# Fused two-block transformer kernel, fp32, one core: first modulation third in the gate-up chunks, gate's steps sooner, shared rotated key as ninth unit, first input tile in halves

## The reference

```python
# first block, DEPTH = 2 times
z = rms_norm(x, g_mix_pre) @ w_in                # 1024 x 3200: rq rk rv rg aq ak av gu gv
y = concat(silu(rg) * retention(rope(rq), rope(rk), rv),
           dilated_attention(rope(aq), rope(ak), av),
           gelu(gu) * (tril(w_s) @ group_norm(gelu(gv)) + b_s))      # "the gate"
x = x + rms_norm(y @ w_out, g_mix_post)
gate, up = split(rms_norm(x, g_ffn_pre) @ w_gate_up)                 # 2816 + 2816 columns
x = x + rms_norm((silu(gate) * up) @ w_down, g_ffn_post)
# second block, l = 0 (even) and l = 1 (odd); the same for ctx, with c_ctx
sh, sc, g = split(silu(c) @ w_mod[l] + b_mod[l], 3)                  # three thirds of 1024
h = rmsnorm(x, norm_g[l]) * (1 + sc) + sh
y = even_layer(h) if l == 0 else odd_layer(h)
x = x + g * y
```

## Time and profile before

| | |
|---|---|
| timed runs, us | 1135.35, 1136.14, 1138.33 |
| profiled execution, us | 1137.99 |
| its span, us | 1136.2 |
| mean granted TensorE clock | 0.986 |
| TensorE (PE) busy | 1085.5, 96% |
| VectorE (DVE) busy | 688.2, 61% |
| ScalarE (ACT) busy | 551.1, 49% |
| GpSimd (POOL) busy | 77.3, 7% |
| moved by DMA | 170.46 MB, mean 150 GB/s |
| chain that ended last | PE 81%, DVE 10%, ACT 4%, issue 3%, DMA 2% |

### The profile page before, as it was taken

One profiled execution on the slowest core, in us unless ns is written; L12 is line 12 of the kernel. 1 busy time (PEld: TensorE's weight loads), 2 busy tenths in 40 slices (PEclk: granted clock), 3 DMA queues, 4 the chain that ended last, 5 costly groups with the idle time before them and its releaser, 6 DMA issues.

```text
span 1136.2 us, 15595 instructions
## 1 busy us (share of the span) xinstructions
PE 1085.5 (96%) x5974; PEld 890.5 (78%) x5974; DVE 688.2 (61%) x1206; ACT 551.1 (49%) x990; POOL 77.3 (7%) x94
## 2 busy tenths in 40 slices
PE   7789999999999989999999999999998999999997
PEld 5588968888886788967888778889796678789785
DVE  5577576666546487575666547523256753876664
ACT  5435455555435435455555445334235742524772
POOL 1000010000001000020000000001000002022040
PEclk9889999999999999999999999999999999999999
DMA  9654467565665754468755485223221011444000
GB/s 333 229 157 135 130 222 241 176 180 183 186 186 195 283 189 131 138 213 278 230 176 181 149 333 150 77 88 103 74 70 42 1 57 56 130 127 133 1 2 38
DMA packets 109572, 170.46 MB, mean 150 GB/s; under 512 B 7213, under 2 KB 70714, under 8 KB 109242
## 3 DMA queue, kind: packets, MB, share of 16 engines
q1 hardware_dynamic: 107424, 161.92, 44.9%
q0 software_dynamic: 1440, 6.10, 1.5%
q10 hardware_dynamic: 634, 1.44, 0.3%
HBM read 168.39 MB, written 1.05 MB: 149 GB/s over the span
## 4 chain that ended last, share of the span: by engine, by line
PE 81%; DVE 10%; ACT 4%; issue 3%; DMA 2%; SPq 0%; DVEq 0%; POOLq 0%; POOL 0%; ACTq 0%
PE PS L478 15%; PE PS L479 15%; PE PS L480 15%; PE PS L2974 4%; PE PS L2975 4%; PE PS L2976 4%; DVE low L451 2%; PE PS L978 2%; DMA raw<-w_in 1%; PE PS L1811 1%; ACT high L441 1%; PE PS L940 1%; PE PS L941 1%; PE PS L942 1%; PE PS L1918 1%
## 5 line engine op out<-in xcount | busy, mean ns | idle before, releaser
L451 DVE TENSOR_TENSOR low<-raw,high 128x1024 fp32r<-128x1024 f32 (+3 forms) x182 | 202.0, 1116 | 224.1 <-ACT high L441 223.5
L478 PE MATMUL PS<-high,hT_high 128*128 128x512 f32 (+2 forms) x796 | 309.6, 389 | 7.8 <-DVE low L451 5.5
L441 ACT ACTIVATE high<-raw 128x1024 fp32r<-128x1024 f32 (+3 forms) x186 | 180.2, 975 | 271.4 <-PE PS L480 148.7
L479 PE MATMUL PS<-low,hT_high 128*128 128x512 f32 (+2 forms) x796 | 301.5, 379 | 0.0
L480 PE MATMUL PS<-high,hT_low 128*128 128x512 f32 (+2 forms) x796 | 301.3, 378 | 0.0
L478 PEld LDWEIGHTS PS<-high,hT_high 128*128 128x128 f32 x796 | 151.8, 191 | 49.1 <-issue 11.4
L480 PEld LDWEIGHTS PS<-high,hT_low 128*128 128x128 f32 x796 | 151.9, 191 | 24.2
L479 PEld LDWEIGHTS PS<-low,hT_high 128*128 128x128 f32 x796 | 152.1, 191 | 22.1
L454 DVE SCALAR_TENSOR_TENSOR low<-raw,vec_cols,high 128x512 fp32r<-128x512 f32 x176 | 124.2, 747 | 51.7 <-ACT high L444 51.7
L444 ACT ACTIVATE high<-raw,vec_cols 128x512 fp32r<-128x512 f32 x176 | 117.0, 714 | 46.6 <-PE PS L480 44.7
L2974 PE MATMUL PS<-high,fT_high 128*128 128x512 f32 x176 | 70.4, 400 | 0.0
(11 more groups left out here) (378 smaller groups left out, 1613.7 us busy)
## 6 DMA issues: line engine op xcount, KB each, us to landing
raw<-w_gate_up SPq DMA_DIRECT2D x176, 256.0 KB
raw<-w_mod SPq DMA_DIRECT2D x48, 512.0 KB
raw<-w_down SPq DMA_DIRECT2D x44, 512.0 KB
raw<-w_in SPq DMA_DIRECT2D x56, 384.0 KB
raw<-o_w_in SPq DMA_DIRECT2D x20, 512.0 KB
raw<-w_out SPq DMA_DIRECT2D x16, 512.0 KB
raw<-e_w_in SPq DMA_DIRECT2D x12, 512.0 KB
raw<-w_in SPq DMA_DIRECT2D x8, 512.0 KB
```

The lines of the kernel that those rows point to most:

```text
L441: last = e.activation(g.high, g.raw, ACT.Copy)
L451: last = e.tensor_tensor(g.low, g.raw, g.high.bitcast(F32), ALU.subtract)
L478: e.matmul(bank, xh[:, k, tokens], g.high[:, i, :], start=first and i == 0, stop=False)
L479: e.matmul(bank, xh[:, k, tokens], g.low[:, i, :], start=False, stop=False)
```

## The change

- The first third of a layer leaves the mixer. Its eight pieces stand singly in the gate-up chunks, one behind each of the four pieces of chunk 2 (`c` = 0) and of chunk 4 (`c` = 1), ScalarE's copies in chunks 3 and 5, the columns at chunk 6, the bias in chunk 7 (MOD_AT).
- The mixer's steps for the gate move forward on ScalarE and VectorE, and aq's low parts move behind the ropes of ak.
- The shared rotated key is turned as the ninth of 17 units and spread while the rest is copied; the cuts of y's pieces 2 and 3 move from step 1 to step 3.
- Piece 2 of the odd layer's first chunk is cut ahead of the context's last tile.
- At the start x's first tile comes in two loads and is taken by halves, the gains from place 5 on are loaded by SyncE, a small activation on ScalarE stands ahead of its other loads, and the positions are worked out after the first pieces.

```diff
-        MOD_AHEAD = {7: (0, 0), 8: (0, 1), 10: (1, 0), 11: (1, 1)}
+        MOD_AT = {(2, h): (0, h) for h in range(4)} | {(4, h): (1, h) for h in range(4)}
...
-                for rows in PAIRS:
+                for h, rows in enumerate(PAIRS):
+                    if (c, h) in MOD_AT:
+                        of, n = MOD_AT[c, h]
+                        add_mod(layer, 0, (of,), PAIRS[n:n + 1])
                     w_gu[layer].add_split(a["w_gate_up"][layer], rows, c * SEQ, SEQ, pre_gain(V_FFN, layer, rows))
...
@@ def mix_step_pe @@
-            if s in MOD_MIX:
-                if s == 6 and where.layer == 0:
-                    e.wait_ge(dve.sem, dve.value("silu_c"))
-                    e.wait_ge(dve.sem, dve.value("wsT"))
-                c, half = MOD_MIX[s]
-                mod_rows_pe(e, 0, c, slice(2 * half, 2 * half + 2))
-            elif s == 11:
+            if s == 11 and where.layer == 0:
+                e.wait_ge(dve.sem, dve.value("wsT"))
+            if s == 11:
                 heads_turn_pe(e, "aq", lambda j: None)
-            elif s == 12:
-                e.wait_ge(act.sem, act.value("mod0_rows1"))
-                for c in range(2):
-                    mod_columns_pe(e, 0, c)
             elif s == 14:
-                e.wait_ge(dve.sem, dve.value("modT0"))
+                if where.layer:
+                    e.wait_ge(dve.sem, dve.value("modT2", layer=where.layer - 1))
                 e.wait_ge(dve.sem, dve.value("gate_norm"))
...
@@ def mix_step_act @@
-            elif s == 5:
                 e.wait_ge(act.sem, act.value("zg1"))
                 e.activation(gel[:, :, :], z_gate[:, :, :], ACT.Square).then_inc(act.sem, act.mark("gel_sq"))
-            elif s == 7:
+            elif s == 6:
...
-            elif s in (8, 11):
-                mod_rows_act(e, 0, int(s == 11))
...
@@ def pe_layer, gate-up @@
+                    if (c, h) in MOD_AT:
+                        of, n = MOD_AT[c, h]
+                        mod_rows_pe(e, 0, of, slice(n, n + 1))
+                    elif (c, h) == (6, 2):
+                        e.wait_ge(dve.sem, dve.value("modT1"))
+                        for of in range(2):
+                            mod_columns_pe(e, 0, of)
...
@@ def mla_take, mla_attention_dve @@
+        MLA_UNITS = (*range(MH), 2 * MH, *range(MH, 2 * MH))
...
+                if n_unit in (11, 12):
+                    k_pe_spread(e, mine, slice(1, 4) if mine is act else slice(4, MH))
...
-                if i == 1:
+                if i == 3:
                     ye_low_dve(e, 2)
                     ye_low_dve(e, 3)
...
@@ def late_act, late_dve @@
             turned_high_act(e, "o_lat", o_full[0], hT, 3)
+            cuts.to(o_in[0].granules[2])
             o_squares_act(e, 3, 1)
...
+            cuts.to(o_in[0].granules[2])
             o_second_half_dve(e, 3)
             o_sum_dve(e, 3)
-            cuts.to(o_in[0].granules[2])
             o_scale_dve(e, 3)
...
@@ start, SyncE and ScalarE @@
-            for t in range(NT):
-                sp.dma_start(x[:, t, :], a["x"].rearrange("b (t p) n -> b p t n", p=P)[0][:, t, :]).then_inc(s_x[t], 16)
+            for j in range(2):
+                sp.dma_start(x[:, 0, 512 * j:512 * (j + 1)], x_in[:, 0, 512 * j:512 * (j + 1)]).then_inc(s_x[0][j], 16)
+            sp.dma_start(x[:, 1, :], x_in[:, 1, :]).then_inc(s_x[1][0], 16)
...
+            vec_loads(sp, GAIN_ROWS[5:])
             sp.dma_start(ws_rows[:, :, :], a["w_s"].rearrange("l g t s -> t (l g) s")).then_inc(s_ws, 16)
...
+            e.activation(small[:, 60:61], half_power[:, 0:1], ACT.Copy)
```

More of the change, by code:

```diff
@@ L357, in add_in @@
             for c in chunks:
-                for h, rows in enumerate(PAIRS):
-                    if 4 * c + h in MOD_AHEAD:
-                        of, half = MOD_AHEAD[4 * c + h]
-                        add_mod(layer, 0, (of,), PAIRS[2 * half:2 * half + 2])
+                for rows in PAIRS:
                     w_in[layer].add(a["w_in"][layer], rows, *IN_COLS[c])
@@ L671, in turned_half, with x_high_act @@
             return PS[:, banks[t][j], :].rearrange("p (k s) -> p k s", s=P), (slice(None), slice(4 * j, 4 * j + 4), slice(t * P, (t + 1) * P))
-        def x_high_act(e, side, t, banks, layer):
-            for j in range(2):
+        def x_high_act(e, side, t, banks, layer, js=range(2)):
+            for j in js:
                 e.wait_ge(pe.sem, pe.value(f"{side}_T{t}{j}", layer=layer))
@@ L688, in mix_gain, with x_low_dve @@
             return vec_cols[:, at:at + 1]
-        def x_low_dve(e, side, t, banks, layer):
-            for j in range(2):
+        def x_low_dve(e, side, t, banks, layer, js=range(2)):
+            for j in js:
                 e.wait_ge(act.sem, act.value(f"{side}_H{t}{j}", layer=layer))
@@ L1615, in mla_turn_pe @@
         def mla_turn_pe(e):
[L1618 to L1620 removed]
+            for n_unit, i in enumerate(MLA_UNITS):
+                bank = n_unit % 8
+                if n_unit < 8:
                     taken(e, "e_kvb", bank // 2)
[L1622 to L1623 removed]
+                else:
+                    mla_taken(e, n_unit - 8)
                 h = i % MH
@@ L2070, in late_act @@
             mla_take(e, act)
-            k_pe_spread(e, act, slice(1, 4))
             mla_attention_act(e)
@@ L2931, in pe_layer @@
                 done.then_inc(granules_done, 1)
+            if layer == 0:
+                e.wait_ge(dve.sem, dve.value("silu_c"))
             mod_rows_pe(e, 1, 0)
```

116 lines of the change are left out of this document (60 added, 56 removed).

## The result

The changed kernel takes 1125.84 us, median of four runs (1124.96 to 1127.42), the kernel before 1136.83 over four (1135.35 to 1138.33): a ratio of 0.9906 with a 95% interval of 0.9891 to 0.9921. It gained 11 us where 21 were forecast, and lies outside the range of 1109 to 1122. The profiled execution took 1126.27 us (before 1137.99), with a span of 1124.5 and a mean clock of 0.995 instead of 0.986.

The account below looks back on a forecast made before the run. TensorE, 96% busy, bounds the kernel; only idle and half-clock time can be won. Terms 10.2 + 5.9 + 2.2 + 3.7 = 22.0, less 1.0 for clock, give 1117.0 profiled and a 1115 us median, range 1109 to 1122.

Parts of the forecast that it names:

- Start, 0.5: Kernel start: first product about 2 us sooner, 0.5 us gained (bounds 0 and 2), the rest a wait for `ws_rows`.
- First layer's mixer, 17.9: First layer up to the end of ak's turn: 17.9 us won, with new waits of 2.9 and 2.6.
- A single piece I take as 0.7, eight 5.8: Gate-up, both layers: eight single pieces 5.8 us plus columns 1.84, 7.7 us put back per layer.
- Rival C: Gate-up chunks 2 and 4 starved of loads: 16.6 us lost per layer, 1148 us; chance 0.03.
- Second layer's mixer, 13.6: Second layer up to the end of ak's turn: 13.6 us won, with a new wait of 2.2.
- Latent attention, 2.2: Shared rotated key and y's cuts: 2.2 us won (bounds 0.5 and 4), wait ahead of y becomes 1.3.
- Odd chunk, 3.7: Odd layer's first chunk: the wait of 2.42 for piece 2's low part and its half clock go, 3.7 us won.
- Clock, "I take off 1.0 in all": Four new or left waits, lengths between 1.83 and 2.38, would each lose 1.7 at half clock; 1.0 us deducted altogether.
- Rival B: Waits move and clock falls again at start, both ak turns and y: gain 15.2, 1121 us; chance 0.15.

Follow-up runs that it names:

- pairs: First third's w_mod pieces used two at a time in the gate-up chunks instead of singly, against the changed kernel: 1117.06 us, 8.8 less.
- one_group: Both row blocks of a first-third piece write to the same 32-partition group, against the changed kernel: 1138.29 us, 12.5 more.
- quads: All four pieces of a half third used together, behind piece 3 of chunks 2 and 4, against the changed kernel: 1118.89 us, 7.0 less.
- start_back: Start's edits undone (x's tile in one load, no early activation, gains by ScalarE, positions at old place), against the changed kernel: 1126.01 us.
- mla_back: Shared rotated key again last of 17 units, y's pieces again cut at step 1, against the changed kernel: 1127.05 us, 1.2 more.
- odd_cut_back: Piece 2 of the odd layer's first chunk cut again behind the context's last tile, against the changed kernel: 1129.51 us, 3.7 more.
- third_back: First third of both layers back in the mixer, new order of the gate's steps kept, against the changed kernel: 1118.85 us, 7.0 less.

## Why the prediction was wrong

- **Start, 0.5.** Right in size as far as can be told: the transposes of `ws_rows` begin 0.7 us sooner (19.36, was 20.05), behind the forecast wait for them (0.28), and undone the start's edits make no measurable difference. The first layer's end is set by VectorE.
- **First layer's mixer, 17.9.** Right, 17.7, though a match to 0.2 is luck where profiles differ by 1.6. The new wait at aq's turn was forecast at 2.9 from 42.9 to 45.75, and is 3.08 up to 46.13. (The 0.8 for ScalarE's table stood there without a row; the load takes 1.28 in the trace, at 31.91, and VectorE's chain idles 0.7 around it.) The second, 2.6 at ak's turn, is 0.21 at 58.61: TensorE reached it at 58.40, not 56.4, 1.5 of that by half clock behind the first wait, and the turn starts with the first of aq's three low parts, not the last. It ended at 60.14, forecast 59.95, because VectorE sets it either way. So the half clock, which the forecast leaves out for this longest of its waits, did no harm here.
- **"A single piece I take as 0.7, eight 5.8".** This is the step that failed. A single piece costs 1.19, as much as a pair, because its two row blocks leave two of the four groups of output partitions empty: 3.7 us too little in each layer; the two stages together fall 7.6 short. (Eight at 0.7 are 5.6, not 5.8; the slip is small beside it.) Shown by the row of the single piece, by the kernel with pairs (8.8 back) and by the one-group kernel (1.90 against 1.05). The rest of the part stood: columns 1.84, copies and bias hidden, loads on time. Rival C got nothing. The queue did not need the forecast's 300 GB/s: TensorE used up chunk 2's eight pieces, 4.19 MB, in 16.3 us (257 GB/s), while the queue moved 177 in that stretch and 293 in chunk 3, and TensorE did not wait: the ring's eight places covered the difference, not a queue at 300. By the estimate from the Trainium skill's DMA: Bandwidth & Descriptors, section Bandwidth, 164 GB/s for single transfers of 512 KB, the chunks would have starved. The trace does not agree, 217 GB/s without a wait; the page's fit is of transfers issued by GpSimd, these are issued by SyncE. Loads did come late with pairs (0.87 in the second layer), with four pieces at once (1.88) and with eight pieces in the mixer.
- **Second layer's mixer, 13.6.** 11.4. VectorE's chain was right to 0.9 (ak's turn ended at 401.51, which with the shift of 6.5 at that point is 408.0 against 407.1). From there the two steps up to the `y_gate` turn took 5.52 us instead of 4.25, 1.3 by half clock. The same stage is 1.6 us shorter in the profiles of `pairs`, `one_group`, `quads` and `start_back`, where the same wait (1.72 to 1.73) left the clock at full: so of the 2.2, 1.6 is clock and 0.6 VectorE's chain. I had sorted 1.83 as a wait that costs no clock; 1.74 was enough in this profile.
- **Latent attention, 2.2.** 1.9 in this trace, but by luck. The wait ahead of y is 2.01, not 1.3, now for VectorE's part of the spread (`kT`, L1408), and the clock stayed; in six other profiles with the same wait it fell, and the stage was no shorter than with the edit undone.
- **Odd chunk, 3.7.** 3.9 in the trace, 3.7 undone. (2.42 and 1.4 to 1.6 less 0.4 are 3.4 to 3.6, not 3.7.)
- **Clock, "I take off 1.0 in all".** As a sum not far off: 1.6 in the second layer's mixer, and in the first it hid inside VectorE's time. As a rule for single waits it failed, and it was not applied as stated: of the four lengths that it names (2.4, 2.6, 2.2 and 1.3) only 2.2 lies between 1.83 and 2.38, and the new wait of 2.9 is not among them. Rival B's gain of 15.2 is nearer to the measured 11 than mine, but for a reason that carries only about a sixth of the difference.

With 1.19 in place of 0.7 and nothing else changed the working gives 1122.4; with the 2.2 of the second mixer as well, 1124.6. What I did not price at all was the choice inside the move: once the gate's order was mended, the third in the mixer cost 7 us less than in single pieces in gate-up and about the same as in pairs.

## What to carry to other kernels

A matmul with 32 weight columns and 512 fp32 columns to stream was priced here by how many output groups ran side by side, not by its count: before splitting such work, ask how many groups each piece fills, and move it in pieces that fill all four. When a change has an order part and a move part, ask what each is worth alone; here the order of the gate's steps on two engines was worth about 12 us and the move, as made, cost 7. When two profiles differ by 1 to 2 us, look first whether the granted clock behind a wait that both have is the same. A busy engine's last result should be one that its consumer can postpone.

## What the runs showed of the hardware

- Two row blocks of 128 x 32 weights by 512 fp32 columns take 1.90 us on one group of 32 output partitions and 1.05 on two; four take 1.07 on four.
- Half clock did not follow the length of the wait alone. The same wait of 1.72 to 1.74 at ak's turn in the second layer was followed by a granted clock of 0.65 to 0.67 over four microseconds in three profiles (the changed kernel, `mla_back`, `odd_cut_back`) and of 1.00 in four (`pairs`, `one_group`, `quads`, `start_back`). The wait of 2.01 to 2.04 ahead of y was followed by 0.57 to 0.64 in six profiles and by 1.00 in five.
- One of 2.29 (`third_back`) and, at the start, one of 2.53 (kernel before, at 12.44) left the clock at full; of the two of 2.38 ahead of y one (`mla_back`) did and one (kernel before) did not. After the first 30 us each of the waits from 2.42 to 5.91 us was followed by half clock for a part of the next four microseconds. What else decides it was not tried.
- Where it fell, half clock cost 1.6 us at ak's turn in the second layer and 1.7 us ahead of y.
